# Expert stage of a hybrid diffusion step: units of 32 tokens on four column groups, experts ranked by count, sixteen weight slots

## The reference

```python
N_EXPERTS, N_EXPERT_GROUPS, TOP_K, D_FF_EXPERT = 16, 4, 2, 512
probs = softmax(t @ w_router); sel = probs + router_bias
best = argmax over 4 groups of the sum of the 2 largest sel in a group
idx = the 2 experts with the largest sel in the best group
combine = gate weights of the 2 chosen experts, normalised
g = einsum("td,edf->tef", t, w_gate); u = einsum("td,edf->tef", t, w_up)
out = einsum("tef,efd->td", silu(g) * u * combine, w_down)
```

## Time and profile before

| | us |
|---|---|
| median of 3 runs | 1047.38 (1044.69 to 1048.4) |
| the profiled execution's own time | 1048.91 |
| its span, first to last instruction | 1047.1 |
| expert stage, first gate matmul to last down matmul | 622.1 to 999.7 |
| after it: copy, store, row gathers, mixing, output | 999.7 to 1047.1 |

### The profile page before, as it was taken

One profiled execution on the slowest core, in us unless ns is written; L12 is line 12 of the kernel. 1 busy time (PEld: TensorE's weight loads), 2 busy tenths in 40 slices (PEclk: granted clock), 3 DMA queues, 4 the chain that ended last, 5 costly groups with the idle time before them and its releaser, 6 DMA issues.

```text
span 1047.1 us, 13807 instructions
## 1 busy us (share of the span) xinstructions
PE 934.5 (89%) x5470; PEld 631.0 (60%) x5470; DVE 360.0 (34%) x620; ACT 168.9 (16%) x350; POOL 217.9 (21%) x256
## 2 busy tenths in 40 slices
PE   2899999998999999999999449999999999999910
PEld 2565655555545555544444348887888877888800
DVE  2330016446755998733225431110111111111128
ACT  5111012112322222200001200010101111000123
POOL 0189996001422333200000000000000000000053
PEclk9989999999999999999999659999999999999965
DMA  8914657323100002840000418989999999999552
GB/s 356 416 81 161 243 216 285 123 81 121 41 1 1 1 1 81 356 189 20 21 20 21 160 41 305 340 327 333 330 326 351 331 327 333 320 347 326 193 215 106
DMA packets 34451, 205.32 MB, mean 196 GB/s; under 512 B 3760, under 2 KB 6384, under 8 KB 16496
## 3 DMA queue, kind: packets, MB, share of 16 engines
q1 hardware_dynamic: 22896, 169.08, 43.7%
q0 software_dynamic: 5472, 20.45, 5.2%
q10 hardware_dynamic: 6048, 15.30, 3.7%
HBM read 184.86 MB, written 19.96 MB: 196 GB/s over the span
## 4 chain that ended last, share of the span: by engine, by line
PE 60%; DVE 10%; issue 2%; DMA 1%; POOL 1%; ACT 1%; ACTq 0%; POOLq 0%; DVEq 0%
PE bank L815 23%; PE bank L711 13%; PE bank L827 11%; PE bank L575 6%; PE bank L800 2%; DVE ex L1355 1%; PE bank L613 1%; DVE xs L1408 1%; DVE ex L1632 1%; PE bank L764 1%; POOL ex L1167 1%; DVE ex L1371 1%; PE bank L677 1%; DVE uT L1649 1%; DMA ex<-slot_out,ri 1%
## 5 line engine op out<-in xcount | busy, mean ns | idle before, releaser
L815 PEld LDWEIGHTS bank<-yT,ex 128*128 128x128 f32 x2176 | 247.0, 193 | 9.0 <-issue 9.0
L815 PE MATMUL bank<-yT,ex 128*128 128x128 f32 x2176 | 247.2, 276 | 1.0 <-DVE yT L1610 1.0
L503 PE MATMUL bank<-hT,ring 128*128 128x512 f32 (+1 forms) x640 | 179.9, 440 | 2.4 <-DMA ring<-w_ring 2.4
L503 PEld LDWEIGHTS bank<-hT,ring 128*128 128x128 f32 x640 | 96.6, 194 | 73.7 <-issue 70.8
L827 PE MATMUL bank<-ex,yT 128*128 128x512 f32 x272 | 120.9, 597 | 0.0
L1617 DVE TENSOR_TENSOR yT<-yT,bank 128x128 f32<-128x128 f32 x68 | 19.6, 288 | 222.8 <-ACT yT L1029 222.8
L827 PEld LDWEIGHTS bank<-ex,yT 128*128 128x128 f32 x272 | 50.3, 190 | 57.8 <-issue 56.9
L575 PE MATMUL bank<-ring,hT 128*128 128x512 f32 x160 | 76.8, 615 | 4.5 <-DVE ex L1379 2.2
L1176 POOL DMA_INDIRECT yT<-h_dram,idx x17 | 17.3, 1017 | 261.7 <-PE bank L800 261.7
L711 PE MATMUL bank<-ring,yT 128*128 128x512 f32 x160 | 70.2, 593 | 0.8 <-DVE yT L1417 0.8
L1167 POOL TENSOR_TENSOR ex<-ex,dts 128x512 f32<-128x512 f32 x40 | 44.3, 1106 | 101.5 <-ACT ex L958 101.4
(11 more groups left out here) (260 smaller groups left out, 955.2 us busy)
## 6 DMA issues: line engine op xcount, KB each, us to landing
ex<-w_exp SPq DMA_DIRECT2D x102, 1024.0 KB, 6.7
ring<-w_ring SPq DMA_DIRECT2D x13, 2048.0 KB, 12.3
yT<-w_late SPq DMA_DIRECT2D x16, 1024.0 KB, 6.4
slot_out<-yT ACTq DMA_DIRECT2D x17, 512.0 KB, 8.7
slot_out<-ex POOLq DMA_DIRECT2D x9, 512.0 KB, 12.9
ex<-x SPq DMA_DIRECT2D x5, 512.0 KB, 7.7
xs<-x SPq DMA_DIRECT2D x5, 512.0 KB, 13.5
y_out<-uT SPq DMA_DIRECT2D x5, 512.0 KB, 2.6
```

The costliest lines, as they stand in the source:

```text
L503: mm = pe.matmul(o, w[:, k, (f % 4) * P:(f % 4 + 1) * P], hT[:, k, lo:hi], start=(k == 0), stop=(k == KT - 1))
L815: mm = pe.matmul(psb[c % 2][:, a * P:(a + 1) * P], w[:, a, k, :], xgT[:, k, :], start=(k == 0), stop=(k == KT - 1))
```

## The change

The work of an expert is cut into units of 32 tokens. A unit's tokens are the stationary operand (32 columns), the weights move: 256 columns in each of four column groups, which write 32 PSUM partitions each. For gate and up a group holds 128 features of both; for down it holds 256 output columns. The weights of gate and up are laid out anew on the host, so that a chunk holds 256 rows of the model width for all features. Between, the activations (32 tokens x 4 groups of 128 features) are multiplied out by ACT and DVE into `ab`, transposed by PE in one 128x128 transpose, and copied by ACT to `aT`.

```diff
+TU = 32
+RANK_UNITS = (4, 5, 4, 4, 4, 4, 3, 3, 3, 3, 3, 3, 2, 2, 2, 2)
+RUN_ORDER = (0, 6, 2, 12, 1, 13, 3, 14, 4, 15, 7, 8, 9, 10, 11, 5)
+LOOP_RANK = RUN_ORDER[-1]
+OVERFLOW = 13
+NSLOT = 16
...
+            def gate_up(v, c, b, u, slot):
+
+                w = slots_[slot].rearrange("p (k g n) -> p k g n", k=2, g=AG)
+                for kk in range(2):
+                    k = 2 * c + kk
+                    for g in range(AG):
+                        mm = pe.matmul(psb[v % 2][g * TU:(g + 1) * TU, 0:256], xgT[b][:, k, u * TU:(u + 1) * TU],
+                                       w[:, kk, g, :], start=(k == 0), stop=(k == KT - 1), skip_group_check=True)
+                return mm
+
+            def turn_act(v):
+                pe.transpose(psb[4][:, 0:P], ab[v % 2], ident).then_inc(s_at, 1)
+
+            def down(v, c, slot):
+
+                w = slots_[slot].rearrange("p (k d) -> p k d", k=2)
+                for kk in range(2):
+                    fb = 2 * c + kk
+                    for g in range(AG):
+                        mm = pe.matmul(psb[6 + v % 2][g * TU:(g + 1) * TU, 0:256], aT[v % 2][:, fb * TU:(fb + 1) * TU],
+                                       w[:, kk, g * 256:(g + 1) * 256], start=(fb == 0), stop=(fb == FT - 1),
+                                       skip_group_check=True)
+                return mm
...
+            for v, (n, q, u) in enumerate(UNITS):
+                if u == TILES[q][1] - 1:
+                    pe.wait_ge(s_xg[(q + 1) % 2], 16 * ((q + 1) // 2 + 1))
+                    pe.wait_ge(s_xgT, 2 * (q + 1))
+                    turn_tokens((q + 1) % 2, TILES[q + 1][1])
...
+                for c in range(4):
+                    m = 6 * n + c
+                    if v == FIRST_V[n]:
+                        pe.wait_ge(s_ch[m % NSLOT], 16 * (m // NSLOT + 1))
+                    mm = gate_up(v, c, q % 2, u, m % NSLOT)
...
+                    if c == 1 and v >= 1:
+                        unit_turn(v - 1)
...
+                if v >= 1:
+                    unit_down(v - 1)
+            unit_turn(NV - 1)
+            unit_down(NV - 1)
```

```diff
+            step(stt(key, counts, float(E), cst[:, C_KEY:C_KEY + E], ALU.mult, ALU.add))
+            step(tt(larger, across(key, E), over(key, E), ALU.is_gt))
+            total(rank, larger)
+            step(tt(is_rank, over(rank, E), across(item, E), ALU.is_equal))
...
+            step(tt(looked, is_rank.unsqueeze(2).to_broadcast([P, E, 3, E]),
+                    table.unsqueeze(1).to_broadcast([P, E, 3, E]), ALU.mult))
+            total(found, looked)
+            base, room_, back = found[:, :, 0], found[:, :, 1], found[:, :, 2]
...
+            step(tt(beyond, counts, room_, ALU.subtract))
+            step(tt(steps, over(beyond, 5), across(cst[:, C_STEP:C_STEP + 5], E), ALU.is_gt))
             total(tiles, steps)
-            step(ts(tiles, tiles, 1.0, None, ALU.add))
...
+            step(tt(moved, within, across(room_, NJ), ALU.is_ge))
+            step(tt(moved, moved, across(shift, NJ), ALU.mult))
+            step(tt(slots, within, across(base, NJ), ALU.add))
+            step(tt(slots, slots, moved, ALU.add))
```

```diff
+            sp.wait_ge(s_own, 1)
+            for n in range(1, E - 1):
+                e = sp.value_load(ri[0:1, RUN_ORDER[n]:RUN_ORDER[n] + 1], min_val=0, max_val=E - 1)
                 for c in range(6):
...
+                    m = 6 * n + c
+                    if m >= NSLOT:
+                        slot_free(m)
+                    sp.dma_start(slots_[m % NSLOT], w_exp[e, c]).then_inc(s_ch[m % NSLOT], 16)
```

Token rows (`xg`), `xgT` and the output tile (`yo`) have two buffers each; the gather of a tile waits for the turn of the tile two before it. A tile's outputs are stored by four DMAs on ACT's queue, one for each column group, in pieces of 256 columns:

```diff
+                for g in range(AG):
+                    act.dma_start(slot_out[rows, g * 256:(g + 1) * 256].rearrange("(u t) c -> t u c", t=TU),
+                                  yo[b][g * TU:(g + 1) * TU, 0:size, :]).then_inc(s_yst[b], 16)
```

The clearing covers the tiles' slots beyond their units and the 13 further tiles, 24 DMAs instead of nine:

```diff
-            for t in range(E, MAX_TILES - 1):
-                pool.dma_start(slot_out[t * P:(t + 1) * P, :], zero_f).then_inc(s_zero, 16)
...
+            for lo, hi in UNFILLED:
+                pool.dma_start(slot_out[lo:hi, :], zero_f[0:hi - lo, :]).then_inc(s_zero, 16)
```

More of the change, by code:

```diff
@@ L46, with slot_tiles, moe_tiles @@
 BIG = 1e30
-MAX_TILES = 26
-SLOTS = MAX_TILES * P
+TU = 32
[4 more added lines that the diff above has]
+NSLOT = 16
+def slot_tiles():
+    first, t = {}, 0
+    for r in [r for r in range(E) if r != LOOP_RANK] + [LOOP_RANK]:
+        first[r] = t
+        t += -(-RANK_UNITS[r] // 4)
+    return first, t
+RANK_TILE, MAIN_TILES = slot_tiles()
+MAX_TILES = MAIN_TILES + OVERFLOW
+SLOTS = MAX_TILES * P
+def moe_tiles():
+    tiles, units = [], []
+    for n, r in enumerate(RUN_ORDER):
+        left, t = RANK_UNITS[r], RANK_TILE[r]
+        while left:
+            size = min(left, 4)
+            if n < E - 1:
+                units += [(n, len(tiles), u) for u in range(size)]
+            tiles.append((t, size))
+            left, t = left - size, t + 1
+    return tiles, units
+TILES, UNITS = moe_tiles()
+NQT = len(TILES) - 1
+NV = len(UNITS)
+LOOP_SLOT = 6 * (E - 1) % NSLOT
+UNFILLED = [(t * P + size * TU, (t + 1) * P) for t, size in TILES if size < 4]
+UNFILLED += [(t * P, (t + 1) * P) for t in range(MAIN_TILES, MAX_TILES)]
+FIRST_V = [next((v for v in range(NV) if UNITS[v][0] == n), NV) for n in range(E)]
+LAST_V = [max((v for v in range(NV) if UNITS[v][0] == n), default=NV) for n in range(E)]
 RING = 3
@@ L1020, in copy_tokens, with copy_act @@
                                ACT.Copy).then_inc(s_xgT, 1)
[L1022 to L1035, removed]
+            def copy_act(v):
+                act.activation(aT[v % 2], psb[4][:, 0:P], ACT.Copy).then_inc(s_aT, 1)
@@ L1568, in _ @@
             dve.wait_ge(s_rk, 1)
-            tiles, ends, base, steps = new(E), new(E), new(E), new(E, 4)
-            step(tt(steps, over(psb[0][:, NJ * E:(NJ + 1) * E], 4), across(cst[:, C_STEP:C_STEP + 4], E), ALU.is_gt))
+            counts = psb[0][:, NJ * E:(NJ + 1) * E]
+            within = psb[0][:, 0:NJ * E].rearrange("p (j e) -> p j e", e=E)
+            item = cst[:, C_ITEM:C_ITEM + E]
+            key, larger, rank, is_rank = new(E), new(E, E), new(E), new(E, E)
+            step(stt(key, counts, float(E), cst[:, C_KEY:C_KEY + E], ALU.mult, ALU.add))
@@ L1575, in _ @@
-            step(ts(base, base, float(P), None, ALU.mult))
-            slots, mine, place = new(NJ, E), new(NJ, E), new(2 * NJ)
-            step(tt(slots, psb[0][:, 0:NJ * E].rearrange("p (j e) -> p j e", e=E), across(base, NJ), ALU.add))
+            step(tt(begin, ends, tiles, ALU.subtract))
+            step(stt(shift, begin, float(P), back, ALU.mult, ALU.subtract))
+            slots, moved, mine, place = new(NJ, E), new(NJ, E), new(NJ, E), new(2 * NJ)
+            step(tt(moved, within, across(room_, NJ), ALU.is_ge))
@@ new lines, in _ @@
+            LB = NQT % 2
+            with dve.Fori(0, k_loop) as i:
+                for w in range(4):
+                    v = NV + w
+                    dve.wait_ge(s_sg, i * 4 + (v + 1))
+                    dve.wait_ge(s_at, i * 4 + (v - 1))
+                    activate(v)
+                    if w >= 1:
+                        dve.wait_ge(s_dn, i * 4 + v)
+                        if w == 1:
+                            dve.wait_ge(s_yst[LB], i * 64 + 64 * (NQT // 2))
+                        copy_out(v - 1, LB, w - 1)
+                dve.wait_ge(s_xtp, i + (NQT + 2))
+                copy_tokens(LB, 4)
+                dve.wait_ge(s_dn, i * 4 + (NV + 4))
+                copy_out(NV + 3, LB, 3)
@@ L1674, in layout @@
     cst[:, C_P4:C_P4 + EG] = EG - np.arange(EG)
-    cst[:, C_ITEM:C_ITEM + 28] = np.arange(28)
-    cst[:, C_STEP:C_STEP + 4] = P * (1 + np.arange(4))
+    cst[:, C_ITEM:C_ITEM + E] = np.arange(E)
+    cst[:, C_STEP:C_STEP + 5] = P * np.arange(5)
+    cst[:, C_KEY:C_KEY + E] = E - 1 - np.arange(E) + 1e5 * (np.arange(E) == 0)
+    first = np.array([RANK_TILE[r] * P for r in range(E)])
+    space = np.array(RANK_UNITS) * TU
+    cst[:, C_TAB:C_TAB + 3 * E] = np.concatenate([first, space, first + space - MAIN_TILES * P])
     cst[:, C_TOKEN:C_TOKEN + 2 * NJ] = p[:, None] + P * (np.arange(2 * NJ) % NJ)
```

336 lines of the change are left out of this document (236 added, 100 removed).

## The result

The changed kernel takes 989.53 us (median of 4 runs, 986.62 to 990.24), the kernel before 1047.22 beside it (4 runs). The ratio is 0.9447, with a 95% interval of 0.9421 to 0.9473. The forecast was 992 us, with 970 to 1032 as range. The profiled execution took 986.62 us, its span is 984.4.

The account below looks back on a forecast made before the run. PE was taken to bound the expert stage, with transfers close behind. Stage -60.9, work before it +5.1 and the end +1.0 sum to -54.8 us, giving 992 us against 1047.38; eight-in-ten range 970 to 1032.

Parts of the forecast that it names:

- packing: Rival for PE's matmuls: column groups pack less densely; three of four side by side make 1080 us; chance 0.08, other slowdowns included.
- transfers: Rival for the expert stage: DMA at 332 GB/s, not PE, ends it, giving 1015 us; chance 0.11.
- stalls: Rival in the expert stage: each unit loses 0.5 to 1 us to ACT's round trip or code loading, 1018 to 1043; chance 0.10.
- the ranks hold: Opposite of a rival in which a token count outgrows its rank's units and extra loop tiles make 1032 us; chance 0.02.
- The unit: PE's work on 32 tokens in the expert stage: 5.8 us, between 5.66 and 5.91, times 51 units.
- The four: Four PE matmul instructions side by side, one per column group: costs what one 256-column instruction does, 0.217 us; 24 a unit.
- Turns of tokens: PE transposes of the next tile's tokens: sixteen before the loop cost 16.0 us, the one in the loop 1.2.
- Stores cost nothing: Expert output stores: four issues on ACT of 0.343 us, followed only by copies PE needs 3 us later; cost nothing.
- Routing: Before the expert stage: ranking the experts adds steps to DVE's path, together 4.6 us.
- First gather: The first fetch of token rows before the expert stage now meets weight loads: 0.5 us, between 0 and 2.5.
- Clearing: POOL, before the stage: 24 DMAs instead of nine, 8.0 us more, hidden by POOL's 80.1 us wait; costs nothing.
- Tail: Kernel end: three more store issues of 0.343 us before the last store lands, +1.0 us.

## Why the prediction was right, and where its terms were not

The forecast said PE would end the stage with 51 units at 5.8 us in about 317 us, and 992 in all. PE ends it, with 51 units, and three rivals fall to runs of their own: packing (on two groups the same work takes twice as long), transfers (their floor lies some 40 us lower, at 401 GB/s, and PE waits for no weights), stalls (a unit is its instructions and 0.40). That the ranks hold is seen in the page's group of DVE's products, 51 where a second round of the loop would add four:

```profile
L1841 DVE TENSOR_TENSOR bcT<-bcT,bank 128x128 f32<-128x128 f32 x51 | 14.6, 287 | 176.3 <-ACT bcT L1182 176.3
```

The terms, from the profiled execution:

- *The unit*, 5.8 us, between 5.66 and 5.91: 5.58, below the lower bound. The four was right (0.217; 0.216). The transpose and its shape changes were 0.40 instead of 0.45, and the handovers, put at 0.14, cost nothing. The lower bound failed because it only let the waits vary and took the 0.34 for shape changes, a difference of two rows with other shapes, as exact. 51 units at 5.575 instead of 5.8 are 11.5 us less.
- *Turns of tokens*: units with one last 6.35, 6.53 or 6.74 us (64, 96 or 128 rows), so 0.77 to 1.16 each; 16 of about 0.95 and one in the loop make 16.3, where 17.2 was said. *Cold start*: 64 + 32 instructions from 629.60 to 636.81 are 2.0 over 3 x 1.73, where 1.65 was said. *Drains*: 1.1 for both instead of 2.0.
- *Stores cost nothing*: wrong by 2.9 us. The step compared the four issues on ACT with the time to the next operand, and gave the stores' bytes room in the transfers, but never set one store's landing against the reuse of its buffer two tiles later. With the one-unit tile of rank 1 between, the buffer was wanted some 7 us after the store's last issue, and the landing took 16.53.
- *Stage in all*: 51 x 5.575 = 284.3, 16.3, 2.0, 1.1 and 2.9 make 306.6 of 306.97 measured; predicted 316.7.
- *Routing*, +4.6: from the last turn ahead of the router to the end of the token numbers it was 25.81 us (587.73 to 613.54) and is 30.42 (585.07 to 615.49), +4.6. The widest of the added steps, priced at 0.98, from the grouped lines of DVE:

```profile
L1785 DVE TENSOR_TENSOR ring<-ring,cst 128x768 f32<-128x768 f32 x1 | 1.0, 958 | 0.0
```

- *First gather*, +0.5, between 0 and 2.5: +4.9 for the way of the data, and 0.85 more before its issue, since POOL loads the loop's count first, which the step didn't count. The prediction had named the cause ("the first gather now meets weight loads") and sized it too small: what it met was ten loads of 1 MB.
- *Clearing*, hidden: POOL's wait behind it went from 80.1 to 70.0, some 10 us where 8.0 was said.

```profile
POOL ex L1351 <- DVE xs L1500: 70.0, 1, 70.0
```

- *Tail*, +1.0: +0.4.

So 992 came near 989.5 in part by luck, because two errors stood against each other: the stage 9.7 us shorter than said, the way to it 5.1 longer. The profiled execution's work ahead of the routing, 2.7 shorter than in the trace of before, is no effect of the change. The sign and the size rest on the four groups, and that term was right. By the Trainium skill, "TensorE: Matmul & The Clock Gate", Part 3 on packing small matmuls, four tiles packed by rows give 3.07 times one and three packed by columns 2.38 times; its table has no row for four column groups. This trace shows no such loss: 0.216 us for four of 256 columns, half of what one of 512 columns took before (0.434), and twice 0.216 when the same four share two groups.

## What to carry to other kernels

Count the work in the pieces that the engine charges for: a tile of 128 slots that holds 33 tokens costs as much as a full one, and smaller stationary pieces on separate column groups cost only a little more for each token (23.5 us for four units with their turn, 22.11 for the old tile), so the gain is the padding left out and nothing else. It holds for these counts: a draw in which an expert outgrows its rank was not run. When a long list of loads is set free at one moment, look which short transfer on the critical path starts just after it, and let that go first. For each output buffer, set the longest landing of a store under full DMA against the shortest time to its reuse, and look for that at the shortest tile.

## What was not expected of the hardware

- A gather of 512 KB took 9.65 us from issue to use among ten loads of 1 MB on another queue, and 4.98 and 4.47 when these waited for it.
- A tile's last quarter, stored in pieces of 1 KB, took 16.53 us to land while the DMA engines were full (share 1.02 from 740.77 to 757.30). The landings of such stores lie far apart: by the view of their line (L1187) the shortest is 1.9 us, the median 8.7, the longest 16.4. Whether the pieces or the loads ahead of it made it so long was not separated.
- Five semaphore waits a unit cost PE nothing when their signal was there before: without the transpose, where all five remain, a unit's 24 fours take 5.18 us, the 0.216 each that eight fours take in the changed kernel.
